# The recurrence's six gate projections run inside the memory attention instead of inside the recurrence

## What is computed

```python
z = rms_norm(x) @ hg_w_in                 # columns q | f | i | g | qm
q, f, i, g = ...                          # 6 heads of 128 each
# gated linear recurrence, 64-token chunks
o = hgrn2(silu(q), lb + (1 - lb) * sigmoid(f), i)
y = rms_norm(o, onorm_g) * silu(g)        # g: the gate projections
# memory attention: 4 heads of 64, 256 memory rows
m = softmax(norm(qm) @ norm(k_mem).T / 8) @ v_mem
x = x + concat([y, m]) @ w_out
```

## Time and profile before

| | |
|---|---|
| time, median of 3 runs | 1918.17 us (1914.97 to 1920.12) |
| the profiled execution | 1913.36 us |
| its span, first to last instruction | 1911.6 us |
| mean granted TensorE clock | 0.954 |
| recurrence, first level matmuls to last output matmul | 641.8 to 779.2 us |
| memory attention, first scores to output projection | 784.7 to 821.1 us |

### The profile page before, as it was taken

One profiled execution on the slowest core, in us unless ns is written; L12 is line 12 of the kernel. 1 busy time (PEld: TensorE's weight loads), 2 busy tenths in 40 slices (PEclk: granted clock), 3 DMA queues, 4 the chain that ended last, 5 costly groups with the idle time before them and its releaser, 6 DMA issues.

```text
span 1911.6 us, 24595 instructions
## 1 busy us (share of the span) xinstructions
PE 1761.6 (92%) x8605; PEld 1427.1 (75%) x8605; DVE 896.7 (47%) x1623; ACT 738.3 (39%) x1122; POOL 703.8 (37%) x362
## 2 busy tenths in 40 slices
PE   6999899996799898798999999989977989999999
PEld 4778566885678787676888888868855768888887
DVE  4587565457522255755444432253355554444200
ACT  4332465223453344414445432134424244544322
POOL 2334111443325565032444444532200324444444
PEclk9999999998899898888999999988988989999999
DMA  4232211242223110012323333322100222333333
GB/s 175 88 110 89 66 34 45 89 132 77 89 67 103 60 48 23 12 56 66 99 88 99 99 99 110 99 72 70 63 12 1 67 66 88 99 99 99 99 100 120
DMA packets 43275, 151.71 MB, mean 79 GB/s; under 512 B 4928, under 2 KB 5056, under 8 KB 43072
## 3 DMA queue, kind: packets, MB, share of 16 engines
q1 hardware_dynamic: 41184, 145.16, 23.8%
q10 hardware_dynamic: 2016, 5.53, 0.8%
HBM read 148.58 MB, written 2.10 MB: 79 GB/s over the span
## 4 chain that ended last, share of the span: by engine, by line
issue 52%; PE 24%; POOL 20%; DVE 1%; ACT 1%; DMA 1%; POOLq 0%; ACTq 0%; DVEq 0%
POOL WL L528 20%; PE DB L607 4%; PE DB L609 4%; PE DB L608 4%; PE SC L893 2%; PE SC L707 1%; PE DB L732 1%; PE DB L657 1%; PE DB L659 1%; PE DB L658 1%; PE OB L721 1%; PE TB L607 1%; PE DB L721 1%; PE OB L919 1%; DMA CONST<-in_consts_dram 1%
## 5 line engine op out<-in xcount | busy, mean ns | idle before, releaser
L528 POOL TENSOR_TENSOR WL<-RAW,WH 128x1024 fp32r<-128x1024 f32 x268 | 647.6, 2417 | 1187.1 <-ACT WH L1090 1187.1
L1090 ACT ACTIVATE WH<-RAW 128x1024 fp32r<-128x1024 f32 x268 | 284.0, 1060 | 794.3 <-PE DB L609 300.3
L960 PE MATMUL DB<-XH,WH 128*128 128x512 f32 x704 | 277.4, 394 | 6.3 <-DVE XL L1499 6.3
L961 PE MATMUL DB<-XL,WH 128*128 128x512 f32 x704 | 275.8, 392 | 0.0
L962 PE MATMUL DB<-XH,WL 128*128 128x512 f32 x704 | 275.6, 391 | 0.0
L607 PE MATMUL DB<-XH,WH 128*128 128x512 f32 (+1 forms) x552 | 231.6, 419 | 14.0 <-DVE XL L1499 9.0
L608 PE MATMUL DB<-XL,WH 128*128 128x512 f32 (+1 forms) x552 | 218.8, 396 | 0.0
L609 PE MATMUL DB<-XH,WL 128*128 128x512 f32 (+1 forms) x552 | 218.1, 395 | 0.0
L960 PEld LDWEIGHTS DB<-XH,WH 128*128 128x128 f32 x704 | 132.9, 189 | 39.3 <-DVE XL L1499 7.5
L962 PEld LDWEIGHTS DB<-XH,WL 128*128 128x128 f32 x704 | 133.3, 189 | 27.9
L961 PEld LDWEIGHTS DB<-XL,WH 128*128 128x128 f32 x704 | 133.3, 189 | 27.1
(11 more groups left out here) (384 smaller groups left out, 3018.4 us busy)
## 6 DMA issues: line engine op xcount, KB each, us to landing
RAW<-in_stream_dram SPq DMA_DIRECT2D x268, 512.0 KB, 3.5
TP<-in_toep_dram ACTq DMA_DIRECT2D x4, 512.0 KB, 3.7
out_dram<-X SPq DMA_DIRECT2D x8, 256.0 KB, 4.3
X<-in_xt_dram ACTq DMA_DIRECT2D x4, 256.0 KB, 5.2
X<-in_xt_dram SPq DMA_DIRECT2D x4, 256.0 KB, 4.7
MRAW<-in_memt_dram ACTq DMA_DIRECT2D x1, 1024.0 KB, 6.9
CONST<-in_consts_dram ACTq DMA_DIRECT2D x1, 448.0 KB, 9.7
MSKI<-in_masks_dram ACTq DMA_DIRECT2D x1, 288.0 KB, 3.6
```

The lines of the kernel that those rows point to most:

```text
L528: nc.gpsimd.tensor_tensor(WL[:, s, :], RAW[:, j, :], WH[:, s, :].bitcast(F32), ALU.subtract).then_inc(lo_done, 1)
L960: mm(o, WH[:, s, c], xh(k), start=(k == 0), stop=False)
L961: mm(o, WH[:, s, c], xl(k), start=False, stop=False)
L1090: A(WH[:, n % SPLIT, :], RAW[:, n % RING, :], ACT.Copy).then_inc(hi_done, 1)
```

## The change

The list `fill` goes. In the recurrence TensorE keeps only the two query projections, beside the first head. `gates_and_spreads` gives the attention's TensorE program six gate k-tiles and one root spread a step: 48 k-tiles in eight steps. The gates accumulate in banks 0 and 4 (`DB[0]` and `TB`), so the attention's scores rotate over two banks instead of four. GpSimd's slab operations leave the recurrence but for the two slabs that stand ready in the ring. ScalarE copies gates 0 to 3 out after the exponentials of pairs 3, 4, 5 and 7 (`gate_out`), runs their Silu after the last of these, and treats gates 4 and 5 after the attention. VectorE first multiplies all heads by their norm in place, one each step, and then by the gates, in three pieces a head; what does not fit into the attention's steps comes after it. A new semaphore `yh_done` tells TensorE's output projection which heads are ready, one after another, where it waited for all six before.

```diff
@@ plan_stream
     for k in range(HG):
-        add(f"hg{k}", 1, 1, KD, "act", (0, 1))
+        add(f"hg{k}", 1, 1, KD, "act", (0, 4))
@@ score banks
-        SCORE = {"ab": (SC[0], SC[1]), "m0": (SC[0], SC[1], TB, DB[0]),
+        SCORE = {"ab": (SC[0], SC[1]), "m0": (SC[0], SC[1]),
@@ GpSimd
-            slabs = [[], [2, 3], [4, 5], [6], [7], [8]]
...
-                    if l == 1:
-                        for n in slabs[h]:
-                            low((s0 + n) % RING, s0 + n)
-            low((s0 + 9) % RING, s0 + 9)
-            lows(s0 + 10, JOBS["uv1"].done + SPLIT)
+                    if h == 1 and l == 1:
+                        low((s0 + 2) % RING, s0 + 2)
+                        low((s0 + 3) % RING, s0 + 3)
+            lows(s0 + 4, JOBS["uv1"].done + SPLIT)
@@ TensorE, recurrence
-                        beside = [feature_tiles(fill.pop(0), xh, xl) for _ in range(2 if h < 2 else 1)]
+                        beside = [feature_tiles(f"qm0{k}", xh, xl) for k in range(2 if h == 0 else 0)]
@@ TensorE, attention
+            def gates_and_spreads():
+                gates = itertools.chain(*(feature_tiles(f"hg{k}", xh, xl) for k in range(HG)))
+                spreads = head_spreads()
+                for k in range(len(segments["m0"])):
+                    for _ in range(6):
+                        next(gates, None)
+                    next(spreads, None)
+                    yield
...
-            attention(segments["m0"], [emptied("hg5"), (hs_std, HEADS["ho5"][0] + 1)], head_spreads())
+            attention(segments["m0"], [(hs_std, HEADS["ho5"][0] + 1)], gates_and_spreads())
...
-                 lambda j: (hs_done, HEADS["ho5"][0] + 1) if j < HG else (o_out, j + 3))
+                 lambda j: (yh_done, j + 1) if j < HG else (o_out, j + 3))
@@ ScalarE
-                    for k in ((0, 1), (2,), (3,), (4,), (5,))[h - 1]:
-                        evac(f"hg{k}", HGT[:, k, :])
...
-                    A(HGT[:, 0:5, :], HGT[:, 0:5, :], ACT.Silu).then_inc(hg_silu, 1)
...
-            attention(segments["m0"])
+            def gate_out(s):
+                k = s["g"] // 2 - segments["m0"][0][0]["g"] // 2
+                for j in range(4):
+                    if s["g"] % 2 and k == 2 + (8 * j + 7) // 6:
+                        evac(f"hg{j}", HGT[:, j, :])
+                        if j == 3:
+                            gates_done(0, 4)
...
+            attention(segments["m0"], gate_out)
+            for j in (4, 5):
+                evac(f"hg{j}", HGT[:, j, :])
+            gates_done(4, 6)
@@ VectorE, head_outputs
-                    link(V.scalar_tensor_tensor(TMP[:, 0, :], HQ[:, h, :], col("onorm"), r, ALU.mult, ALU.mult))
-                    yield
-                    link(V.tensor_tensor(TMP[:, 1, :], TMP[:, 0, :], HGT[:, h, :], ALU.mult))
+                    V.scalar_tensor_tensor(HQ[:, h, :], HQ[:, h, :], col("onorm"), r, ALU.mult, ALU.mult).then_inc(hs_done, 1)
+                    for _ in range(4):
+                        yield
+                dve.wait_ge(hs_done, HEADS["ho5"][0] + 1)
+                for h in range(HG):
+                    dve.wait_ge(hg_silu, 1 if h < 4 else 2)
+                    link(V.tensor_tensor(TMP[:, 1, :], HQ[:, h, :], HGT[:, h, :], ALU.mult))
                     yield
                     link(V.tensor_copy(YH[:, h, :], TMP[:, 1, :]))
                     yield
-                    V.tensor_tensor(YL[:, h, :], TMP[:, 1, :], YH[:, h, :].bitcast(F32), ALU.subtract).then_inc(hs_done, 1)
-                    dve.wait_ge(hs_done, HEADS[f"ho{h}"][0] + 1)
+                    V.tensor_tensor(YL[:, h, :], TMP[:, 1, :], YH[:, h, :].bitcast(F32), ALU.subtract).then_inc(yh_done, 1)
+                    dve.wait_ge(yh_done, h + 1)
                     yield
```

More of the change, by code:

```diff
@@ L409, in build @@
         hg_silu = sem("hg_silu")
+        yh_done = sem("yh_done")
         reset_ready = sem("reset_ready")
@@ L872, in _ @@
                 token_job(f"hv{k}", xh, xl, 384)
-            fill = ["qm00", "qm01"] + [f"hg{k}" for k in range(HG)]
             n = 0
@@ L920, in _ @@
                 last.then_inc(ho_mm, 1)
-            assert not fill
             def head_spreads():
@@ L1347, in _, with gates_done @@
                 else:
-                    for k in ((0, 1), (2,), (3,), (4,), (5,))[h - 1]:
-                        evac(f"hg{k}", HGT[:, k, :])
-                if h:
                     head_out(h - 1)
                 if h == 4:
-                    act.wait_ge(act_emptied, EMPTIED[JOBS["hg4"].banks[0]][1])
-                    A(HGT[:, 0:5, :], HGT[:, 0:5, :], ACT.Silu).then_inc(hg_silu, 1)
                     group_std("qm0", 1.0, 1)
             head_out(HG - 1)
-            act.wait_ge(act_emptied, EMPTIED[JOBS["hg5"].banks[0]][1])
-            A(HGT[:, 5, :], HGT[:, 5, :], ACT.Silu).then_inc(hg_silu, 1)
             group_std("ho", 1.0 / P, 0)
-            attention(segments["m0"])
+            def gate_out(s):
[5 more added lines that the diff above has]
+                            gates_done(0, 4)
+            def gates_done(a, b):
+                act.wait_ge(act_emptied, EMPTIED[JOBS[f"hg{b - 1}"].banks[0]][1])
+                A(HGT[:, a:b, :], HGT[:, a:b, :], ACT.Silu).then_inc(hg_silu, 1)
+            attention(segments["m0"], gate_out)
+            for j in (4, 5):
+                evac(f"hg{j}", HGT[:, j, :])
+            gates_done(4, 6)
             def tail(l, ni):
@@ L1800, in head_outputs @@
             def head_outputs():
-                dve.wait_ge(hg_silu, 2)
                 group_roots("ho")
@@ L1821, in _ @@
                 query_norm(k)
-            attention(segments["m0"], head_outputs())
+            outputs = head_outputs()
+            attention(segments["m0"], outputs)
+            for _ in outputs:
+                pass
             def tail(l, ni, gain):
```

## The result

The changed kernel takes 1923.07 us (median of 15 runs, 1920.37 to 1927.15) against 1918.04 us for the kernel before (15 runs beside them, 1907.89 to 1920.39): a ratio of 1.0038, 95% interval 1.0024 to 1.0053. By the medians it is slower by 5.0 us. The ratio is that of the means (1923.5 and 1916.2 us, so +7.4), which differ by more because three of the 15 runs of before lie at 1908 us. The forecast was +12, 1930 us. The profiled execution has a span of 1918.6 us, 7.0 above that of before.

A forecast was written before the change was run, and what follows sets the result against it. TensorE was taken to bound most stages, including the full-clock heads, with room in the attention; -18 us in the recurrence and +30 in the attention gave +12 on the 1918.2 median, 1930 us, range 1910 to 1946.

The forecast's parts named there:

- Removed, full clock: Heads two to six: without gate tiles a head takes 15.3 us from 18.3 (second 16.0) at 2.4 GHz; 33 us gained.
- The Silu's hole: Between fifth and sixth head: Silu and its table go, the remaining 3 us on ScalarE is covered, costed at nothing.
- The clock: Heads two to six: TensorE's clock falls in levels, returns at each head's end; heads 18.3 us, second 19.3; gain 18.
- The rule on the clock: Recurrence: brief, frequent TensorE idling swings its clock, so it gains 18 us, total +12; otherwise 33 and -3.
- Added to the attention: Memory attention: 48 gate k-tiles, 32.7 us of TensorE work, plus waits; stage 36.4 to 66.6 us, 30 lost.
- the slab waits: Attention: TensorE waits for late-split slabs of the third and sixth gates, 1.7 and 2.4 us.
- The last wait: After the attention: output projection waits for VectorE's last two gated heads, about 1 us, left out of the sum.
- The stretch ahead of the attention: Before the attention: keeps its 5.5 us, hanging on the square root of the last head sum, not the Silu.
- the full clock: Rival, heads two to six: level matmuls keep TensorE at 2.4 GHz; -3 us, 1915, at best 1909; chance 0.27.
- A feed late at every gate: Rival, attention: ScalarE splits each slab a step later, TensorE waits 3 us more for four slabs; +12, 1942; chance 0.10.
- an attention that grows by 25 us only: Rival, attention: slab and end waits hide, stage +25; with alternating clock +7, 1925; no separate chance given.
- The low clock throughout: Rival, heads two to six: TensorE's clock stays down without wide matmuls, heads 23 us; +36, 1954; chance 0.12.

The follow-up runs named there:

- e2: The changed kernel plus one 512-column matmul, result unused, after each of the first eight levels of heads two to six: 1914.31 us, 0.9990 of before.
- e3: The changed kernel plus two one-column products, results unused, after each of the first eight levels of heads two to six: 1955.34 us (one run).
- e7: The kernel before with its Silu behind the recurrence, only the sixth gate moved into the attention, two score banks: 1904.46 us, 0.9931 of before.
- e1: The changed kernel with three slabs (third gate, sixth gate, output projection's first) split one step earlier by ScalarE: 1922.59 us, 1.0034 of before.
- e5: The kernel before with the first memory attention's scores on two PSUM banks instead of four: 1915.51 us, 0.9991 of before.
- e8: The kernel before with its Silu behind the recurrence and ten unused 512-wide matmuls between fifth and sixth head: 1904.27 us, 0.9938 of before.
- e9: e7 plus unused 512-wide matmuls, ten between fifth and sixth head and thirteen ahead of the attention: 1897.89 us, 0.9889 of before.
- e6: The changed kernel with both the earlier slab splits of e1 and the extra wide matmuls of e2: 1915.37 us, 0.9985 of before.
- e4: The kernel before with the five-head Silu taken out from between fifth and sixth head; one Silu over six follows the recurrence: 1908.57 us, 0.9963 of before.

## Why the prediction came out as it did

The direction was right. The size was too large, by 3 us in the three stages, 5 in the span and 7 in the medians. Of the mechanism, the heavier attention was right. Heads whose clock falls in the levels and comes back at the end were right for the fourth and the fifth head; in the other three the clock did something else. Against the sum:

- *Removed, full clock.* I gave a head 15.3 us; the two at 1.00 took 15.7 and 15.4. The second head, put at 16.0, took 16.7 at 1.00 with e2's extra matmuls. The sixth copy-out came 7.1 us into the head and the last products 7.6, where I had 6.7 and 7.0, and 0.4 more for the head sum.
- *The Silu's hole.* Costed at nothing once the Silu is gone, and nothing was left.
- *The clock.* This is the term that was mis-sized. I put four heads at 18.3 and the second at 19.3, 92.5 in all; they took 87.7. In heads four and five the clock did what I said, falling in the levels and coming back ahead of the output matmuls (17.9 and 17.8). In the second, which I had too low, it fell within the first 4 us and came back only at 689.5, in the last of the output matmuls (0.53 from 687.6 to 689.7): 20.9. In the third and the sixth it didn't fall at all. I had taken one value, from between 15.3 and 23, for heads of three kinds, and that their sum comes within 5 us is in part luck. The gain was 22.7, not 18.
- *The rule on the clock.* The Trainium skill (TensorE: Matmul & The Clock Gate, section A second HAM failure mode: psum-queue depth-cycling) says that short, frequent idle times between groups of matmuls make the clock swing. In 3 of 5 heads it does swing, but the idle times are in the other two: the third and the sixth, with 2.6 to 3.0 us without TensorE work, stayed at 1.00, the second and the fourth fell after 0.3 us each, and e3 lost the clock with hardly any. So the trace doesn't bear out idle time as the cause here. A window of before in the earlier trace rows, too, was at 1.00 with 40% idle. Why the third and sixth head escape, and the sixth one of e7, is open; e1's profile has the same pattern of heads as the changed kernel's, to 0.1 us, which speaks against chance from run to run; with one execution of each it isn't excluded.
- *Added to the attention.* 67.2 us against 66.6 in the forecast. A pair took 7.00 (about 7), the slab waits 1.6 and 2.4 (1.7 and 2.4), the end 2.8 (3.5). The score banks, costed at nothing, make TensorE wait 1.7 us in the first pairs, and e5 has 1.6 for them alone: a cover that holds in the middle of a stage doesn't yet at its start. The sum didn't suffer, by luck: I had 2 us of idle time in just these pairs, for another reason. And TensorE was busy for 86% of the stage (58.55 of 67.70 us), not over 90.
- *The last wait, left out at "about 1 us".* It was 1.3, and it stands in the output projection's 47.3 for 46.1.
- *The stretch ahead of the attention* kept its length: 5.4 against 5.5.

With 23.0 in place of 18, 30.8 in place of 30 and 1.2 more behind, the same sum gives +9.0, which is what the three stages show. From there to +7.0 of span is the rest (-2.0). From +7.0 to +5.0 of median it is where the profiled executions lie: that of before 4.7 below its median, that of the changed kernel 2.7 below. I had put the +12 on the median as if both lay alike. The rivals: the full clock's condition didn't hold in three heads, and where e2 forced it, the result was no change that can be told from noise (0.9990; +2.1 us in the stages) where it said -3. The 1909 named for its best case doesn't follow from the 3.5 us beside it, which give 1911.7. A feed late at every gate didn't come (two waits on GpSimd, of the size forecast), nor an attention that grows by 25 us only. The low clock throughout came nearly true in the second head (mean clock 0.59, 20.9 us against its 23) and in no other: at the end of the third to the sixth the output matmuls ran at 1.00.

What e7 adds is why the change loses at all. The room in the attention was real, 1.1 us a pair, and one tile of 0.68 fits into it: 1.4 us for the gate. With six it is used up, and a gate costs 30.8 / 6 = 5.1 us there, nearly its 5.4 of matmuls (32.7 / 6). In the third to the sixth head a gate cost less than that where it stood, 18.3 - 15.6 = 2.7 us at the full clock, because half of it filled TensorE's waits for VectorE; only the second one of the second head cost its full price and more, 6.3. So by these prices five of the six were better left where they were. The 5.1 has the slab waits (4.0 us), the last one (2.8) and those for two score banks (1.7) in it; e1 removes the first two and gives most of it back in the output projection.

## What to carry to other kernels

Work that fills the gaps between short dependent steps can be what keeps TensorE at 2.4 GHz, so count what the steps cost at 1.2 GHz before moving it away. Where only an empty wait is left, a few wide matmuls that compute nothing can pay (e8, e9). Move into a stage no more than its measured idle time per step holds. And when an edit is worth less than the rest of the kernel scatters by, compare stages between marks in the trace, in more than one kernel or execution.

## What the runs showed of the hardware

- In e3, with products of 64 columns and one column and TensorE's record 97% busy, the mean granted clock of the five heads was 0.56 to 0.69. In e2, with one 512-column matmul more per level than in the changed kernel, it was 1.00 in all five (e6 too).
- A wait of 2.4 us without TensorE work was followed by a fall of the clock in e4 (next head 24.8 us), and not in e7 (18.3). Ten wide matmuls in it prevented the fall in e8; in e9 thirteen more, ahead of the attention, took the clock of its first 8 us from 0.50 (e7) to 1.00.
- VectorE operations of 0.34 and 0.69 us took 2.17 and 2.73 when GpSimd's weight remainder had started 0.5 and 0.2 us before them.
- Work far from any edit took 1681.7 to 1692.6 us in eleven profiled executions, and whole executions of one kernel differed by up to 12.5 us (before: 1907.9 to 1920.4). What sets this was not tried.
